# Hybrid decoder layer on one core: the three copies of the sample cache in the queries-and-keys stage wait for later tiles, and a stage's semaphores are cleared behind GpSimd's first work

## The chip, the cores and the metric

The kernel runs on one core of one Trainium2 chip. The metric is the device time of one execution in microseconds (us); lower is better. The times shown are those of three runs of the kernel before; the profile comes from one more execution of it.

## What is computed

One layer of a decoder trunk, in float32, over a prompt of 2048 tokens and a sample of 8 x 4 tokens, of width 1024. What matters here:

```python
h = rms_norm(x, norm1_g) * (1 + sc1) + sh1
z = h @ w_in                                     # q, k, v: 512 columns each; u: 1024
q = rms_norm(q.reshape(B, T, 8, 64), q_norm_g)   # per head
k = rms_norm(k.reshape(B, T, 8, 64), k_norm_g)
o_attn, new_k, new_v = attend(q, k, v)           # three dilated window patterns
...                                              # gated causal convolution of 31 taps on u
x = x + g1 * (concat([o_attn, o_conv]) @ w_o)
x = x + g2 * (square(relu(h2 @ w_ff1)) @ w_ff2)
# sample: the window after appending, an output of the layer
k_all = concatenate([cache_k_l, k], axis=1); new_k_sample = k_all[:, -2048:]
v_all = concatenate([cache_v_l, v], axis=1); new_v_sample = v_all[:, -2048:]
```

The two caches are 8 x 2048 x 512 floats each. All but the first four rows of each sequence go to the output shifted by four rows: 16 copies from DRAM to DRAM, 4088 KB each.

## The kernel before, in words

The program is a row of stages, each a block of its own with one instruction stream per engine: modulation and biases, values and the gated input (VU), queries and keys (QK), prompt attention (PA), sample attention (SA), mixing (MX), feed-forward (FF). A block ends with a barrier over all five engines. GpSimd gathers the other four, releases them, and then clears the semaphores of what has ended (`clear_ended`, L132 to L136: for each range of numbers a drain of GpSimd and a range clear). The other engines don't wait for that.

**Queries and keys** (L1187 to L1460) works tile by tile, 17 tiles: first the 32 sample tokens, then 16 tiles of 128. A float32 product is made of three passes over operands split into a high and a low part.
- TensorE: `products(u)` (L1413 to L1415), 48 matmuls in two halves, each of which adds one to `z_pe`, so that tile u is done at z_pe of 2 (u + 1); behind them `turn_qk(u - 2)` (L1445), 8 transposes of a normed tile into `t_ps`, which wait until ScalarE has taken the turned tile before (`t_done`).
- ScalarE: squares, scaling by head (L1315), then `turned_queries` (L1279) and `turned_keys` (L1291, L1292), which copy turned queries and keys to the buffer `qkT` of two slots. They wait until the store of the tile two before has left its slot (`t_out`).
- VectorE: the norms (L1346 and following), the key gain (L1381), and 9 to 10 us a tile of the prompt's convolution (L307).
- SyncE: for each tile the loads of both parts of h of three tiles on (L1194, 512 KB each), the store of the keys (L1200, 256 KB), the stores of the turned tile (L1214 `qt_d`, L1217 `kt_d`, 192 KB each), and for eight tiles one early load for the next stage (L1238: bias rows, then values of 256 or 1024 KB). It waits in the order in which these stand.
- GpSimd: the sample's convolution, 62 small operations one after the other (L1258 to L1262), then the fourth, fifth and sixth copy of the cache (`copy_cache`, L168 to L174), each behind a wait for `z_pe`. Then it has nothing to do until the stage ends.

**Feed-forward** (L2944 and following) starts with weights and part of h loaded. ScalarE splits off the high part of slot after slot of weights (`high`, L3217) and of h (L3226). GpSimd makes the low parts of the weight slots (`low(s)`, L3159) and of four pieces of h (`h_low(0, 3)`, L3168), VectorE those of four other pieces (L3350) and then the sums for the fast products (L3367 to L3380). TensorE waits for the low part of each slot (`w_lod`) before its matmuls (L3683 to L3685).

Of the kernel before, what the change touches and what calls it, by code (L numbers as in the profile page):

```python
# [94 lines left out]
def build(nc, I, O):  # L95
# [24 lines left out]
    with whole:  # L120
# [11 lines left out]
        def clear_ended():  # L132

            if ended_sems:
                nc.clear_and_free_semaphores(list(ended_sems))
                ended_sems.clear()  # L136
# [31 lines left out]
        def copy_cache(eng, n):  # L168

            b = n // 2  # L170
            for name, out in ((("cache_k", "new_k_sample"), ("cache_v", "new_v_sample"))[n % 2],):
                src = I[name][0, b].rearrange("r h d -> (r h d)")[DS * AW:WINC * AW]
                dst = O[out][0, b].rearrange("r h d -> (r h d)")[0:(WINC - DS) * AW]
                eng.dma_start(dst.rearrange("(a n) -> a n", a=16), src.rearrange("(a n) -> a n", a=16)).then_inc(copied, 16)  # L174
# [62 lines left out]
        with conv:  # L237
# [104 lines left out]
            with ExitStack() as st:  # L342
# [65 lines left out]
                with nc.Block() as block:  # L408
                    @block.gpsimd
                    def _(pool):  # L410
                        pool.memset(ident[:], 0.0).then_inc(id_zero, 1)
                        pool.wait_ge(id_zero, 1)
                        pool.affine_select(out=ident[:], in_=ident[:], compare_op=ALU.not_equal, fill=1.0, base=0,
                                           pattern=[[-1, P]], channel_multiplier=1).then_inc(id_done, 1)
                        pool.wait_ge(tb_done, 3)
                        pool.dma_start(brow_d, biasB[:]).then_inc(tb_out, 16)
                        for g in range(3, NTB):
                            cols = table_cols(g)
                            pool.wait_ge(tb_done, g + 1)
                            pool.dma_start(sbias_d[:, cols], biasS[:, g % 2, 0:cols.stop - cols.start]).then_inc(ps_out[g % 2], 16)  # L420
                        pool.wait_ge(tb_out, 16)
                        pool.wait_ge(ps_out[0], 16 * 2)
                        pool.wait_ge(ps_out[1], 16 * 2)
# [717 lines left out]
            with ExitStack() as st:  # L1141
# [45 lines left out]
                with nc.Block() as block:  # L1187
# [62 lines left out]
                    @block.gpsimd  # L1250
                    def _(pool):
                        step = Chain(pool, tap_d)
                        pool.wait_ge(w_lod, KT)
                        view = lambda t: t[:].rearrange("p c (b t) -> p c b t", t=DS)
                        for j in range(TAPS):
                            w = tapT[:, j * CC:(j + 1) * CC].unsqueeze(2).unsqueeze(3).to_broadcast([P, CC, DB, DS])
                            if j == 0:
                                step(pool.tensor_tensor(view(dwS), gluS[:, :, :, j:j + DS], w, ALU.mult))  # L1258
                                step(pool.tensor_tensor(dwS[:], dwS[:], vecT[:, V_CB:V_CB + CC].unsqueeze(2).to_broadcast([P, CC, NS]), ALU.add))
                            else:  # L1260
                                step(pool.tensor_tensor(view(dwT), gluS[:, :, :, j:j + DS], w, ALU.mult))
                                step(pool.tensor_tensor(dwS[:], dwS[:], dwT[:], ALU.add))  # L1262
                        pool.sem_inc(dw_done, 1)
                        for i in (2, 5, 8):
                            pool.wait_ge(z_pe, 2 * i)
                            copy_cache(pool, 3 + i // 3)

                    @block.scalar
                    def _(act):
# [1402 lines left out]
        with ExitStack() as st:  # L2672
# [147 lines left out]
            def slot_source(eng, s):  # L2820

                b, i = locate(s)
                if b >= BLKS:
                    r = (s - S_OWN) % RAW
                    eng.wait_ge(raw_in[r], 16 * sum(raw_loads(n) for n in range(S_OWN + r, s + 1, RAW)))
                    return flat_glu[:, r * 512:(r + 1) * 512]
                if i < up_slots(b):
                    j, o = divmod(i, PAIR_SLOTS[b])
                    b11, b21, b12, b22 = raw_up(b, j)
                    if is_plain(b):  # L2830
                        raw_ready(eng, b * 4 + j)
                        return (b11, b21, b12, b22)[o]
                    if o in (0, 2, 6):
                        raw_ready(eng, b * 4 + j)
                    else:
                        eng.wait_ge(t_d, 4 * pair_number(b, j) + {4: 1, 3: 2, 1: 3, 5: 4}[o])
                    return (b11, wT[:, 1], b21, wT[:, 2], wT[:, 0], wT[:, 3], b22)[o]
                k = i - up_slots(b)
                U = b * 4 + 2 + k // 4
                raw_ready(eng, U)  # L2840
                return ff_raw[:, U % 2].rearrange("p (f c) -> p f c", f=FB)[:, :, (k % 4) * P:(k % 4 + 1) * P]

            def slot_view(t, s):
                v = t[s % WR]
                b, i = locate(s)
                return v if i < up_slots(b) or b >= BLKS else v.rearrange("p (f c) -> p f c", f=FB)
# [55 lines left out]
            def h_pieces(run, g):  # L2902
                return [(run * HG + g) % 2 * 4 + n for n in range(4)]
# [36 lines left out]

            FIN = {0: 0, 2: 1, 6: 2, 8: 3, 12: 4, 13: 5}

            clear_ended()
            with nc.Block() as block:  # L2944
                @block.sync
                def _(sp):
# [205 lines left out]
                @block.gpsimd  # L3152
                def _(pool):
                    def low(s):
                        if s >= NSLOT:
                            return
                        pool.wait_ge(w_hid, s + 1)
                        src = slot_source(pool, s)
                        pool.tensor_tensor(slot_view(w_lo, s), src, slot_view(w_hi, s).bitcast(F32), ALU.subtract).then_inc(w_lod, 1)  # L3159

                    def h_low(run, g):
                        w = RUNS[run][1]
                        o = {1: 4, 3: 5}[g]
                        for n in range(4):
                            i = h_pieces(run, g)[n]
                            h_ready(pool, run, g, n)
                            pool.wait_ge(ahh_d, 16 * run + 4 * g + n + 1)
                            pool.tensor_tensor(h_lo[o][n][:, 0:w], h_raw[:, i, 0:w], h_hi[o][n][:, 0:w].bitcast(F32), ALU.subtract).then_inc(ahl_p, 1)  # L3168

                    def a_low(e):  # L3170
                        f, tok, w = a_place(e)
                        n = LOW0[e // 8] + e % 8
                        pool.wait_ge(ahi_d, n + 1)
                        pool.wait_ge(sq_d, e + 1)
                        pool.tensor_tensor(a_lo[:, f, tok], z[e % 4][:, 0:w], a_hi[:, f, tok].bitcast(F32), ALU.subtract).then_inc(alo_d, 1)  # L3175

                    def last_low(b):

                        w = RUNS[b // BLKS][1]
                        pool.wait_ge(ahi_d, LOW0[b] + 14)  # L3180
                        pool.tensor_tensor(operand(a_lo, s_lo, "S4", 1, w), seven_source("S4", 1)[:, 0:w],
                                           operand(a_hi, s_hi, "S4", 1, w).bitcast(F32), ALU.subtract).then_inc(alo_d, 1)

                    pool.sem_inc(w_lod, 1)
                    pool.sem_inc(ahl_p, 4)
                    low(1)
                    h_low(0, 3)
                    for s in range(2, WR):
                        low(s)
                    for b in range(NB_ALL):  # L3190
                        run, blk = divmod(b, BLKS)
                        for i in range(up_slots(b)):
                            j, o = divmod(i, PAIR_SLOTS[b])
                            e = 8 * b + 4 * j
                            if is_plain(b):
                                low(SLOT0[b] + i + WR)
                                if o % 2:
                                    a_low(e + o - 1)
                                    a_low(e + o)
                                continue  # L3200
                            low(SLOT0[b] + i + WR)
                        for k in range(DOWN_SLOTS[b]):
                            if blk == BLKS - 1 and run < NR - 1 and k in (1, 3):
                                h_low(run + 1, k)
                            if SEVEN[b] and k == 8:
                                last_low(b)
                            low(SLOT0[b] + up_slots(b) + k + WR)
# [612 lines left out]
```

## Time and profile before

| | |
|---|---|
| median of three runs | 2605.22 us (2602.17 to 2607.79) |
| the profiled execution's own time | 2604.63 us |
| its span in the trace | 2602.8 us |
| TensorE, VectorE, ScalarE, GpSimd busy | 97%, 72%, 49%, 50% of the span |
| mean granted clock of TensorE | 0.985 of full speed |

All times in rows are microseconds from the start of the span. In the profile PE is TensorE (PEld its weight loads), DVE VectorE, ACT ScalarE, POOL GpSimd, SP SyncE; a q behind the name is the engine's instruction queue. The queries-and-keys stage lies at 384 to 610, feed-forward begins at 1237.

### The profile page before, as it was taken

The numbers are of one execution on the slowest core, as the hardware profiler recorded it, in microseconds if no ns is written. First come the engines' busy times: TensorE is split into PE (matmuls) and PEld (weight loads), VectorE is DVE, ScalarE is ACT, GpSimd is POOL, SyncE is SP. The second block draws the span as 40 slices with busy tenths as digits, with TensorE's granted clock in tenths as the row PEclk, the third lists the DMA queues.
The fourth block names the chain that finished last, engine by engine and source line by source line (L and its number), as shares of the span: only waits on it lengthen the run. The fifth ranks groups of instructions, "written<-read, shape, count | busy, mean of one in ns | idle before, by whom it ended". The sixth has DMA issues, their size and how long they took to land. (4 is left out here: it accounts for less than half of the span.)

```text
span 2602.8 us, 46423 instructions
## 1 busy us (share of the span) xinstructions
PE 2515.0 (97%) x16058; PEld 2231.9 (86%) x16058; DVE 1879.3 (72%) x4104; ACT 1281.9 (49%) x3185; POOL 1306.6 (50%) x920
## 2 busy tenths in 40 slices
PE   7999999899999889999899999999999999999998
PEld 4788867687777646887899999999999999999998
DVE  4268898797999647877866666666767786667776
ACT  3443324457888624655434443434555554455553
POOL 0000006006999205664655555556777775677773
PEclk8999999899999999999999999999999999999999
DMA  7866524953445794664456666665555657565443
GB/s 300 289 215 236 205 97 161 302 154 117 136 138 163 271 351 154 190 216 139 150 179 250 235 242 228 211 215 164 183 191 178 193 182 237 167 198 159 144 141 126
DMA packets 362197, 507.84 MB, mean 195 GB/s; under 512 B 29338, under 2 KB 277894, under 8 KB 352102
## 3 DMA queue, kind: packets, MB, share of 16 engines
q1 hardware_dynamic: 340090, 455.45, 53.2%
q0 software_dynamic: 4272, 39.19, 4.3%
q10 hardware_dynamic: 17604, 10.24, 1.3%
q8 instruction: 131, 2.15, 0.3%
q14 instruction: 100, 0.82, 0.1%
HBM read 405.10 MB, written 171.81 MB: 222 GB/s over the span
## 5 line engine op out<-in xcount | busy, mean ns | idle before, releaser
L3159 POOL TENSOR_TENSOR ff_w_lo<-gluT,ff_w_hi 128x512 fp32r<-128x512 f32 x450 | 626.7, 1405 | 319.2 <-ACT ff_w_hi L3217 317.1
L3217 ACT ACTIVATE ff_w_hi<-gluT 128x512 fp32r<-128x512 f32 x450 | 278.7, 626 | 271.6 <-PE ff_u_ps L3685 168.6
L3683 PE MATMUL ff_u_ps<-ff_a_hi,ff_w_hi 128*128 128x352 f32 (+1 forms) x696 | 223.4, 321 | 3.7 <-POOL ff_a_lo L3175 2.5
L3685 PE MATMUL ff_u_ps<-ff_a_hi,ff_w_lo 128*128 128x352 f32 (+1 forms) x696 | 223.0, 320 | 0.0
L3684 PE MATMUL ff_u_ps<-ff_a_lo,ff_w_hi 128*128 128x352 f32 (+1 forms) x696 | 222.5, 320 | 0.0
L1810 ACT ACTIVATE pa_score<-pa_score,pa_stat 128x256 f32<-128x256 f32 (+1 forms) x384 | 172.3, 451 | 30.2 <-DVE pa_stat L1752 27.9
L3683 PE MATMUL ff_u_ps<-ff_h_hi,ff_w_hi 128*128 128x352 f32 (+1 forms) x548 | 176.0, 321 | 1.6 <-DVE ff_u L3567 0.8
L3685 PE MATMUL ff_u_ps<-ff_h_hi,ff_w_lo 128*128 128x352 f32 (+1 forms) x548 | 175.2, 320 | 0.0
L3684 PE MATMUL ff_u_ps<-ff_h_lo,ff_w_hi 128*128 128x352 f32 (+1 forms) x548 | 174.9, 319 | 0.0
L307 DVE SCALAR_TENSOR_TENSOR vu_dwp<-gluT,tapT,vu_dwp 128x512 f32<-128x512 f32 x240 | 161.1, 750 | 0.8 <-DVE rstd L215 0.8
L1025 PE MATMUL vu_z_ps<-vu_w_hi,last_hi 128*128 128x512 f32 (+1 forms) x384 | 152.0, 396 | 0.7 <-DVEq L963 0.7
L1026 PE MATMUL vu_z_ps<-vu_w_lo,last_hi 128*128 128x512 f32 (+1 forms) x384 | 150.3, 392 | 0.0
L1027 PE MATMUL vu_z_ps<-vu_w_hi,last_lo 128*128 128x512 f32 (+1 forms) x384 | 150.0, 391 | 0.0
L3683 PEld LDWEIGHTS ff_u_ps<-ff_a_hi,ff_w_hi 128*128 128x128 f32 x696 | 130.8, 188 | 4.6 <-POOL ff_a_lo L3175 3.0
L3684 PEld LDWEIGHTS ff_u_ps<-ff_a_lo,ff_w_hi 128*128 128x128 f32 x696 | 131.1, 188 | 0.0
L3685 PEld LDWEIGHTS ff_u_ps<-ff_a_hi,ff_w_lo 128*128 128x128 f32 x696 | 130.7, 188 | 0.0
L3159 POOL TENSOR_TENSOR over_acc<-gluT,over_dwq 128x512 fp32r<-128x512 f32 x75 | 104.6, 1395 | 37.1 <-ACT over_dwq L3217 36.4
L3683 PE MATMUL opening_ps<-ff_a_hi,ff_w_hi 128*128 128x352 f32 (+1 forms) x368 | 118.1, 321 | 0.9 <-POOL ff_a_lo L3175 0.9
L3685 PE MATMUL opening_ps<-ff_a_hi,ff_w_lo 128*128 128x352 f32 (+1 forms) x368 | 117.9, 320 | 0.0
L3684 PE MATMUL opening_ps<-ff_a_lo,ff_w_hi 128*128 128x352 f32 (+1 forms) x368 | 117.7, 320 | 0.0
L1650 POOL TENSOR_SCALAR pa_tap_x<-gluT,tapT 128x1024 f32<-128x1024 f32 x40 | 113.9, 2847 | 3.0
L2616 PE MATMUL mx_z_ps<-mx_wo_hi,mx_m_hi 128*128 128x512 f32 (+1 forms) x272 | 110.5, 406 | 0.0
(565 smaller groups left out, 7735.3 us busy)
## 6 DMA issues: line engine op xcount, KB each, us to landing
gluT<-in_w_ff_dram SPq DMA_DIRECT2D x196, 256.0 KB, 3.5
gluT<-in_w_ff_dram SPq DMA_DIRECT2D x64, 512.0 KB, 5.2
gluT<-tu_d SPq DMA_DIRECT2D x112, 256.0 KB, 3.5
gluT<-td_d SPq DMA_DIRECT2D x96, 256.0 KB, 3.2
out_new_k_sample_dram<-in_cache_k_dram SPq DMA_DIRECT2D x40, 511.0 KB, 5.2
out_new_v_sample_dram<-in_cache_v_dram SPq DMA_DIRECT2D x40, 511.0 KB, 5.6
dwq<-in_w_ada_dram SPq DMA_DIRECT2D x32, 512.0 KB, 9.3
gluT<-in_cache_k_dram SPq DMA_DIRECT2D x16, 1024.0 KB, 8.7
```

Source lines behind the costliest of these rows:

```text
L307: return v.scalar_tensor_tensor(out=out, in0=x, scalar=tap(j, c), in1=out, op0=ALU.mult, op1=ALU.add)
L1025: pe.matmul(z, hi, w_hi[:, k, cols], start=k == 0, stop=False)
L1026: pe.matmul(z, hi, w_lo[:, k, cols], start=False, stop=False)
L1027: mm = pe.matmul(z, lo, w_hi[:, k, cols], start=False, stop=k == KT - 1)
L1650: step(pool.tensor_scalar(tap_x[:], gluT[:, c, j + SEQ - LATE:j + SEQ], tap(j, c), None, ALU.mult))
L1810: act.activation(prob[:, u % 4, hh, cols], score[:, u % 4, hh, cols], ACT.Exp, bias=stat[:, p, t, 0, h:h + 1], scale=-1.0, accum_out=stat[ ...
L2616: pe.matmul(z_ps[c][0:n], hi, wo_hi[:, k, cols], start=k == 0, stop=False)
L3159: pool.tensor_tensor(slot_view(w_lo, s), src, slot_view(w_hi, s).bitcast(F32), ALU.subtract).then_inc(w_lod, 1)
L3217: act.activation(slot_view(w_hi, s), src, ACT.Copy).then_inc(w_hid, 1)
L3683: pe.matmul(out, w_hi[s % WR][:, w], hi, start=first, stop=False, skip_group_check=more)
L3684: pe.matmul(out, w_hi[s % WR][:, w], lo, start=False, stop=False, skip_group_check=more)
L3685: return pe.matmul(out, w_lo[s % WR][:, w], hi, start=False, stop=last, skip_group_check=more)
```

## The change

Two edits. In the queries-and-keys stage the waits ahead of the three copies of the cache go from z_pe of 4, 10 and 16 (two, five and eight tiles' products) to 8, 14 and 20 (four, seven and ten tiles'). In feed-forward the clearing of the ended semaphores is no longer emitted ahead of the block but inside GpSimd's stream, behind `low(1)` and `h_low(0, 3)`.

```diff
                         pool.sem_inc(dw_done, 1)
-                        for i in (2, 5, 8):
+                        for n, i in enumerate((4, 7, 10)):
                             pool.wait_ge(z_pe, 2 * i)
-                            copy_cache(pool, 3 + i // 3)
+                            copy_cache(pool, 3 + n)
...
             FIN = {0: 0, 2: 1, 6: 2, 8: 3, 12: 4, 13: 5}
 
-            clear_ended()
             with nc.Block() as block:
...
                     pool.sem_inc(ahl_p, 4)
                     low(1)
                     h_low(0, 3)
+                    clear_ended()
                     for s in range(2, WR):
                         low(s)
```

No engine's instructions change their order in the queries-and-keys stage; only the numbers that the three waits compare with do. This is GpSimd's end of that stage (qk_dwS is the sample's convolution), before and now alike:

```order
L1261 TENSOR_TENSOR qk_dwT<-gluS,tapT 128x128
L1262 TENSOR_TENSOR qk_dwS<-qk_dwS,qk_dwT 128x128
L174 DMA out_new_v_sample_dram<-in_cache_v_dram 64x16352
L174 DMA out_new_k_sample_dram<-in_cache_k_dram 64x16352
L174 DMA out_new_v_sample_dram<-in_cache_v_dram 64x16352
L1187 UNCONDITIONAL_BRANCH
L135 ISA
```

The three copies stand one behind the other, with the stage's end right behind them.

GpSimd at the seam from mixing to feed-forward, of before (ISA at L135 is a range clear, ff_w_lo a weight slot's low part, ff_h_lo a piece of h's):

```order
L2322 DMA x1_d<-mx_x1 32x1024
L2221 UNCONDITIONAL_BRANCH
L135 ISA x2
L3152 UNCONDITIONAL_BRANCH
L3159 TENSOR_TENSOR ff_w_lo1<-gluT,ff_w_hi1 128x512
L3168 TENSOR_TENSOR ff_h_lo<-gluT,ff_h_hi 128x352 x4
L3159 TENSOR_TENSOR ff_w_lo2<-gluT,ff_w_hi2 128x512
L3159 TENSOR_TENSOR ff_w_lo3<-gluT,ff_w_hi3 128x512
```

The same place in the changed program, where the lines of the stage have numbers lower by one up to the new call:

```order
L2322 DMA x1_d<-mx_x1 32x1024
L2221 UNCONDITIONAL_BRANCH
L3151 UNCONDITIONAL_BRANCH
L3158 TENSOR_TENSOR ff_w_lo1<-gluT,ff_w_hi1 128x512
L3167 TENSOR_TENSOR ff_h_lo<-gluT,ff_h_hi 128x352 x4
L135 ISA x2
L3158 TENSOR_TENSOR ff_w_lo2<-gluT,ff_w_hi2 128x512
L3158 TENSOR_TENSOR ff_w_lo3<-gluT,ff_w_hi3 128x512
```

The two clears, each with its drain, moved from ahead of the first weight slot to between the four pieces of h and the second slot; the other engines' streams are as they were.

## Rows read from the trace of the kernel before

**Rows 1.** The page, busy time: engine, us (share), instructions.
```profile
PE 2515.0 (97%) x16058; PEld 2231.9 (86%) x16058; DVE 1879.3 (72%) x4104; ACT 1281.9 (49%) x3185; POOL 1306.6 (50%) x920
```

**Rows 2.** Windows of a tile's length: busy time by engine, granted clock, DMA share, GB/s.
```profile
458.40:470.20 11.80, 10.09 (x45) 8.02 (x43) 11.23 (x22) 0.00 (x0) 0.00 (x0) 1.00 0.91 307
470.20:482.00 11.80, 2.68 (x11) 2.51 (x12) 1.23 (x2) 4.20 (x20) 0.00 (x0) 0.54 1.00 319
...
505.60:517.40 11.80, 11.80 (x58) 9.87 (x57) 10.52 (x20) 4.78 (x20) 0.00 (x0) 1.00 0.86 290
```

**Rows 3.** Timeline of TensorE, L1445: start, us, what, [idle before, releaser].
```profile
456.56 1.03 PE L1445 MATMUL qk_t_ps<-ident,qk_nrm 128*128 128x128 f32 x8
...
479.32 1.94 PE L1445 MATMUL qk_t_ps<-ident,qk_nrm 128*128 128x128 f32 x8 [10.84 <-ACT qk_qkT L1292]
...
493.76 1.03 PE L1445 MATMUL qk_t_ps<-ident,qk_nrm 128*128 128x128 f32 x8
...
505.57 1.03 PE L1445 MATMUL qk_t_ps<-ident,qk_nrm 128*128 128x128 f32 x8
```

**Rows 4.** Timeline of ScalarE, turned queries and keys.
```profile
477.80 0.58 ACT L1279 ACTIVATE qk_qkT<-qk_t_ps,qk_qgain 128x384 f32<-128x384 f32 x1 [19.81 <-DMA kt_d<-qk_qkT]
...
478.68 0.50 ACT L1292 ACTIVATE qk_qkT<-qk_t_ps 128x384 f32<-128x384 f32 x1
...
513.21 0.58 ACT L1279 ACTIVATE qk_qkT<-qk_t_ps,qk_qgain 128x384 f32<-128x384 f32 x1 [6.85 <-DMA kt_d<-qk_qkT]
```

**Rows 5.** Timeline of GpSimd, the three copies as issued.
```profile
446.44 0.56 POOL L174 DMA_DIRECT2D out_new_v_sample_dram<-in_cache_v_dram  x1 [0.63 <-POOL qk_dwS L1262]
447.01 0.50 POOL L174 DMA_DIRECT2D out_new_k_sample_dram<-in_cache_k_dram  x1
494.22 0.50 POOL L174 DMA_DIRECT2D out_new_v_sample_dram<-in_cache_v_dram  x1 [46.71 <-PE qk_z_ps L1415]
```

**Rows 6.** Timeline of SyncE's queue: start, us that the issue took.
```profile
451.08 0.50 SPq L1217 DMA_DIRECT2D kt_d<-qk_qkT  x1
...
457.12 14.62 SPq L1194 DMA_DIRECT2D qk_third_lo<-hs_d  x1
...
476.18 0.63 SPq L1217 DMA_DIRECT2D kt_d<-qk_qkT  x1
```

**Rows 7.** DMA issues near 446.4, 447.0, 476.2, 494.0 and 494.2: size, us to landing.
```profile
out_new_v_sample_dram<-in_cache_v_dram POOLq DMA_DIRECT2D x1, 4088.0 KB, 17.6
...
out_new_k_sample_dram<-in_cache_k_dram POOLq DMA_DIRECT2D x1, 4088.0 KB, 29.4
...
kt_d<-qk_qkT SPq DMA_DIRECT2D x1, 192.0 KB, 7.3
...
last_hi<-hs_d SPq DMA_DIRECT2D x1, 512.0 KB, 3.5
...
out_new_v_sample_dram<-in_cache_v_dram POOLq DMA_DIRECT2D x1, 4088.0 KB, 16.3
```

**Rows 8.** Instructions of L135 from 1236 to 1240: ns min/median/max, first and last start.
```profile
L135 POOLq DRAIN  x2: 71/78/86, 1237.1 to 1237.4; - x2
L135 POOLq EVENT_SEMAPHORE_RANGE_CLEAR  x2: 109/164/218, 1237.2 to 1237.5; - x2
```

**Rows 9.** Timelines of ScalarE, GpSimd, TensorE and VectorE at feed-forward's start.
```profile
1237.32 0.63 ACT L3217 ACTIVATE ff_w_hi<-gluT 128x512 fp32r<-128x512 f32 x1 [5.46 <-PEq L2221]
...
1238.04 1.26 POOL L3159 TENSOR_TENSOR ff_w_lo<-gluT,ff_w_hi 128x512 fp32r<-128x512 f32 x1 [7.56 <-ACT ff_w_hi L3217]
...
1244.29 7.13 POOL L3159 TENSOR_TENSOR ff_w_lo<-gluT,ff_w_hi 128x512 fp32r<-128x512 f32 x5
...
1245.62 0.43 PE L3683 MATMUL ff_u_ps<-over_dwq,ff_w_hi 128*128 128x352 f32 x1 [0.44 <-POOL ff_w_lo L3159]
...
1283.32 0.43 PE L3683 MATMUL ff_u_ps<-ff_a_hi,ff_w_hi 128*128 128x352 f32 x1 [1.27 <-DVE ff_y L3515]
...
1246.31 0.89 DVE L3367 TENSOR_TENSOR ff_e<-gluT 128x352 f32<-128x352 f32 x1 [4.59 <-DMA gluT<-h_d]
```

## Prediction

> **What bounds the kernel now.** I read the page's part on busy time first: TensorE is busy 2515.0 of 2602.8 us [rows 1], so nearly all of what can be won lies in the 88 us in which it stands still or runs slowly, and the question is whether the change touches any of them. The view of waits for the queries-and-keys stage names the line, and the windows of 11.8 us (one tile) show it: from 458.4 TensorE is busy 10.09 of 11.80, from 470.2 only 2.68 at a granted clock of 0.54, where a later tile has 11.80 at 1.00 [rows 2]. The timeline has the cause to the microsecond. TensorE turns a tile's queries and keys (L1445) after each tile of products; undisturbed tiles follow each other in 505.57 - 493.76 = 11.81 us. After 456.56 the next turn was due at 468.4. It began at 479.32, after 10.84 us of idling for ScalarE's L1292, and the one after it at 493.76 [rows 3]. Two tiles took 37.20 us where 23.62 are due: **13.6 us are lost**, 10.9 by standing still and 2.7 because the tile after it began at the lower clock.
>
> ScalarE was not slow: it waited 19.81 us, until 477.80, for a store of turned keys to leave its buffer, and then needed until 479.18 (478.68 + 0.50) [rows 4]. That store was issued at 451.08 and took 26.7 us; SyncE's own queue stood for 14.62 us from 457.12 [rows 6]. What lay ahead of it are two copies of the sample cache, 4088 KB each, issued at 446.44 and 447.01 [rows 5]. They landed 17.6 and 29.4 us later, at 464.0 and 476.4 [rows 7]; the store came free 1.4 us after the second.
>
> Why two at once? The copies stand behind the sample convolution on GpSimd, and that ends only when the first one is issued, at 446.44. By then the waits for z_pe of 4 and 10 (two and five tiles' products; the fifth's ended about 444.8) are long met, so neither holds anything, and only the third copy has a wait of its own, 46.71 us, until 494.22 [rows 5].
>
> **The change, part by part.** *Copies.* The waits become z_pe of 8, 14 and 20, met when the fourth, seventh and tenth tile's products end. In a stage without the loss the products end where the turns begin: 456.56 - 2 x 11.8 = 433.0, 468.4 and 503.8. The first wait is still passed before the convolution ends, so the first copy stays at 446.44. The second moves from 447.01 to 468.4. The third moves by the program's count of tiles two later, from 494.22 to 503.8. Nothing is queued behind them on GpSimd but the end of the stage.
>
> What is left at the first place: one copy. The trace has that case, the third copy: alone, issued at 494.22, it landed after 16.3 us, at 510.5 [rows 5, 7]. ScalarE was then let go at 513.21, after a wait of 6.85 us [rows 4], 19.0 us after the copy's issue, and TensorE lost nothing (11.80 busy of 11.80 from 505.6) [rows 2]. The same 19.0 us after 446.44 give 465.4; ScalarE takes 1.4 us (477.80 to 479.18) and is done at 466.8, 1.6 us ahead of the turn due at 468.4. With the 17.6 us landing in place of 16.3 it is 468.1, just in time. So I take the whole stall as gone: **-13.6**. The second and third copy stand in the same place of a tile as the third does now; by the same 19.0 us ScalarE is free at 487.4 and done at 488.8, against a turn due at 492.0, and for the third at 522.8 and 524.2 against 527.4: **0** each, with 3.2 us to spare. The bounds of this part: 0 gained if the stall merely moves, -13.6 if it goes; a larger gain has no row behind it. The stage's other engines follow TensorE's pace in the undisturbed windows, so I expect the whole of it to reach the end.
>
> *Clearing.* The two drains and two range clears cost 2 x 78 + 2 x 164 ns = 0.48 us, with the gaps between them about 0.6: in front of the block they run from 1237.1 to about 1237.7 [rows 8], while GpSimd has nothing to do: its first work begins at 1238.04, 0.09 us after ScalarE's L3217 ended (1237.32 + 0.63) [rows 9]. So taking them away there gains **0**; the cover is ScalarE's first split. Behind `h_low(0, 3)` they stand ahead of the split of slot 2, at 1244.29, and TensorE does wait for that split: 0.44 us, until 1245.62 [rows 9]. There they cost up to +0.6, since GpSimd runs without a gap up to it. But TensorE stops once more at 1283.32, for 1.27 us, for VectorE, whose chain starts at 1246.31 with a load that was issued ahead of where the clearing now stands [rows 9], so a shift of 0.6 is taken up there. Bounds 0 and +0.6; I take **0**, nearer to the row at 1283.32, and keep +0.6 for the range.
>
> **Sum.** 2604.63 (the profiled execution's own time) - 13.6 + 0 = **2591.0 us**. The median of the three runs shown is 0.6 higher, 2605.22, and they spread over 5.6 us. A difference within 0.2% (5.2 us) can't be told from none.
>
> **A rule weighed.** The store came free only with the copies ahead of it, though it is 192 KB on another queue; a load issued 0.27 us ahead of the third copy landed in 3.5 us [rows 7]. The Trainium skill (DMA: Bandwidth & Descriptors, section Queues, rings and completion order) says that each DMA engine goes round-robin between queues, a packet at a time. By that alone a small store would share the engines and not wait for a copy to end, one copy or two, and pulling the copies apart would change nothing: 2604.6. The trace speaks against it, since the store's release follows the last copy's landing at both places, by 1.4 and 2.7 us.
>
> **Rivals.** *The second copy meets the backlog of the first.* While the copy runs, SyncE is held. Now the following tile's keys are stored at 476.18, 0.2 us before the last copy's landing, and take 7.3 us [rows 6, 7]. With the landing at 462.7 to 464.0 that store goes out at about 462.5 to 463.8 and lands at 469.8 to 471.1, and the second copy is issued at 468.4, in the middle of it. If it is caught it is freed at 487.4, ScalarE is done at 488.8, TensorE's turn due at 480.2 is 8.6 late and the clock costs 2.7: 11.3 of the 13.6 are given back, **2602.3**. For it: the margin is negative. Against it: the load that was issued only 0.27 us ahead of a copy was not caught, and this store is 4.6 us ahead. *Small stalls.* The first copy's margin of 1.6 us is missed, or the 1 MB load of the values takes up the others' 3.2: a stall of 1 to 3 us at one to three places, with slow matmuls after each, **2594 to 2600**. *Nothing changes*, because what a store waits for is SyncE's own backlog (loads of 512 KB and the bias rows), not the number of copies: **2604.6**; against it stands the 26.7 us beside two copies and the shorter wait beside one. *Slower.* The three copies, now spread, each stop TensorE: that takes a store's release more than 22.2 us after the copy's issue at the second and third (19.0 today; the turns are due 23.6 us after it, less ScalarE's 1.4). If each costs what the pair costs now, 3 x 13.6 - 13.6 = +27.2, **2631.8**; with a release a few us over the margin it is some 2610. For it: the values' 1 MB load now runs into the second copy. It needs the landing to be 3 us worse twice, against which stand the 16.3 and 17.6 us of two different places.
>
> **How the numbers follow.** The forecast has 0.74, small stalls 0.08, the caught store 0.07, nothing changes 0.05, slower 0.06. Faster by over 0.2% are the first two: 0.82. Within 0.2%: 0.12. Slower: 0.06. The forecast's own range is 2591.0 with +0.6 for the clearing and about 2.8 us to each side for the spread of runs. Taking in the small stalls gives 2587.5 to 2600.0, which holds 0.82.
>
> **What would show it.** Right: GpSimd's second copy issued near 468.4 and its third near 503.8; L1445 at 456.6, 468.4, 480.2 without an idle row for L1292; granted clock 1.00 from 446.6 on; ScalarE waits of about 7 us for kt_d behind each copy; the stage's last turns and everything behind them 13.6 us earlier; GpSimd's clearing at about 1230.7, with TensorE's wait for slot 2 grown from 0.44 to about 1.0, and its wait for VectorE 38 us later shrunk. Wrong: a wait of TensorE for L1292 at 480.2 (the caught store), or after all three copies.

## The result and the profile after

The changed kernel takes **2587.06 us**, median of five runs (2586.98 to 2593.3), beside 2602.17 for the kernel before in five runs on the same chip (2599.52 to 2607.79). The ratio is 0.9943 [0.9928, 0.9958]. Faster was right, and the forecast of 2591.0 is 3.9 us too high; the measured median lies 0.4 us below the lower end of the range, 2587.5. The profiled execution took 2586.98 us, its span 2585.2.

TensorE's busy time by the page, against [rows 1]:

```profile
PE 2510.4 (97%) x16058; PEld 2229.0 (86%) x16058; DVE 1884.0 (73%) x4104; ACT 1283.0 (50%) x3185; POOL 1302.1 (50%) x920
```

The windows of a tile's length in queries and keys, against [rows 2] (busy us and instructions of PE, PEld, DVE, ACT, POOL, then granted clock, DMA share, GB/s):

```profile
458.40:470.20 11.80, 11.80 (x58) 9.86 (x57) 11.23 (x21) 5.87 (x24) 0.50 (x1) 1.00 1.07 340
470.20:482.00 11.80, 11.80 (x58) 9.86 (x57) 11.23 (x21) 5.75 (x22) 0.00 (x0) 1.00 1.25 435
482.00:493.80 11.80, 11.80 (x58) 9.86 (x57) 11.23 (x21) 4.31 (x20) 0.00 (x0) 1.00 0.82 270
```

The window from 470.2, in which TensorE was busy 2.68 us at a clock of 0.54, now has 11.80 at 1.00. The turns of L1445 on TensorE's timeline, against [rows 3]:

```profile
457.24 1.03 PE L1445 MATMUL qk_t_ps<-ident,qk_nrm 128*128 128x128 f32 x8
...
469.01 1.03 PE L1445 MATMUL qk_t_ps<-ident,qk_nrm 128*128 128x128 f32 x8
...
480.78 1.03 PE L1445 MATMUL qk_t_ps<-ident,qk_nrm 128*128 128x128 f32 x8
...
492.56 1.03 PE L1445 MATMUL qk_t_ps<-ident,qk_nrm 128*128 128x128 f32 x8
```

They follow each other in 11.77 to 11.78 us with no bracket (idle time and what ended it) behind them, so none waited. GpSimd's copies, against [rows 5], and ScalarE's waits for the store of turned keys, against [rows 4]:

```profile
443.38 0.56 POOL L174 DMA_DIRECT2D out_new_v_sample_dram<-in_cache_v_dram  x1 [0.62 <-POOL qk_dwS L1262]
469.48 0.50 POOL L174 DMA_DIRECT2D out_new_k_sample_dram<-in_cache_k_dram  x1 [25.55 <-PE qk_z_ps L1415]
504.79 0.50 POOL L174 DMA_DIRECT2D out_new_v_sample_dram<-in_cache_v_dram  x1 [34.80 <-PE qk_z_ps L1415]
```

```profile
464.46 0.58 ACT L1279 ACTIVATE qk_qkT<-qk_t_ps,qk_qgain 128x384 f32<-128x384 f32 x1 [5.93 <-DMA kt_d<-qk_qkT]
...
489.49 0.58 ACT L1279 ACTIVATE qk_qkT<-qk_t_ps,qk_qgain 128x384 f32<-128x384 f32 x1 [7.91 <-DMA kt_d<-qk_qkT]
```

The second and third copies stand within 1.1 us of 468.4 and 503.8. ScalarE still waits behind them, but its work is done before TensorE needs it.

**Where the time went.** Cut at the barriers between stages (us; Q/K is queries and keys):

```
                        before  before,again  after  after,again
modulation                65.3      63.2       65.1     65.0
values and updates       318.8     316.7      318.8    319.5
Q/K                      225.7     224.7      212.9    212.5
prompt attention         273.0     272.6      272.7    272.7
sample attention          79.8      80.3       78.1     78.4
mixing                   274.5     274.5      271.0    274.6
feed-forward            1365.7    1365.8     1366.6   1366.7
```

The spans differ by 17.6 us, and only 12.8 of these are in the stage where the copies stand; feed-forward gives 0.9 back. Of the rest, 3.5 are mixing's. That isn't the change's: the changed kernel, profiled again, has 274.6 there, and three kernels below that keep the stall (three copies at once, later early loads, copies at the second, sixth and ninth tile) have 270.9 to 271.4. Sample attention's 1.7 isn't either: these three have 78.2 to 78.3, and one kernel with the copies spread has 80.7. Mixing's 3.5 us all lie in its first 38 us. There the kernel before waits for a load of the output weights. TensorE's timeline, kernel before:

```profile
969.02 5.40 PE L2645 MATMUL opening_ps<-gluT 128*128 128x512 f32 x8 [2.12 <-DMA gluT<-in_w_o_dram]
```

The changed kernel waits 0.78 us at this line, for ScalarE. The load is thus part of the difference; the granted clock, 0.68 from 969.0 to 974.4 beside 1.00 in the changed kernel's matching stretch from 952.2, goes with another 1.7. Why the load came late isn't shown.

A pair of profiles thus makes the gain look 5.7 us larger than what the two places of the change give (12.8 - 0.9 = 11.9).

### The profile page after: what moved, and what is told of

The parts are those of the page before. It is cut to its first block and busy times, and to the rows that moved or that the text cites. A ratio compares the mean times of both kernels' runs of the same rounds, so it can differ in the third digit from the quotient of the medians.

```text
span 2585.2 us, 46423 instructions
## 1 busy us (share of the span) xinstructions
PE 2510.4 (97%) x16058; PEld 2229.0 (86%) x16058; DVE 1884.0 (73%) x4104; ACT 1283.0 (50%) x3185; POOL 1302.1 (50%) x920
## 5 line engine op out<-in xcount | busy, mean ns | idle before, releaser
L3683 PE MATMUL ff_u_ps<-ff_a_hi,ff_w_hi 128*128 128x352 f32 (+1 forms) x696 | 223.3, 321 | 3.8 <-POOL ff_a_lo L3174 2.5
L3684 PE MATMUL ff_u_ps<-ff_a_lo,ff_w_hi 128*128 128x352 f32 (+1 forms) x696 | 222.5, 320 | 0.0
L3683 PE MATMUL ff_u_ps<-ff_h_hi,ff_w_hi 128*128 128x352 f32 (+1 forms) x548 | 176.0, 321 | 1.7 <-DVE ff_u L3567 0.8
L3683 PEld LDWEIGHTS ff_u_ps<-ff_a_hi,ff_w_hi 128*128 128x128 f32 x696 | 130.8, 188 | 4.6 <-POOL ff_a_lo L3174 3.1
L3683 PE MATMUL opening_ps<-ff_a_hi,ff_w_hi 128*128 128x352 f32 (+1 forms) x368 | 118.1, 321 | 0.9 <-POOL ff_a_lo L3174 0.9
```

Of the source, the lines that this page charges most:

```text
L3683: pe.matmul(out, w_hi[s % WR][:, w], hi, start=first, stop=False, skip_group_check=more)
L3684: pe.matmul(out, w_hi[s % WR][:, w], lo, start=False, stop=False, skip_group_check=more)
```

## The experiments

Twelve runs: ten kernels, and the two of the comparison once more. Edits are against the kernel before or after, as said. Each ratio is to the kernel before on the same chip.

**One part at a time.** The copies alone (after, with the clearing back in front) and the clearing alone (before, with the clearing moved):

```
 e1: after, with   + clear_ended()          ahead of feed-forward's block
                   -     clear_ended()      behind h_low(0, 3)
 e2: before, with  - clear_ended()          ahead of feed-forward's block
                   +     clear_ended()      behind h_low(0, 3)
```

> The later waits of the three copies alone; the clearing stays ahead of feed-forward. Theory (the whole gain is the copies'; the clearing costs a little): 13 to 15 us less than before, ratio 0.9942 to 0.9950; the queries-and-keys stage about 212.9 us from barrier to barrier as in the changed kernel, feed-forward 1365.7 as in the kernel before, so 0.9 us faster there than the changed kernel. Rival (the clearing brings part of the 15.1): only some 10 to 12 us less, and mixing back at 274.5 us.

> The moved clearing alone; the copies wait as before. Theory: the 13.6 us stall is there (10.8 us idle before the turn at 479), feed-forward 0 to 1 us longer, time 0 to 1 us over before, ratio 1.000 to 1.0004. Rival (the clearing brings part of the gain): 2 to 5 us less than before.

Measured: copies alone 2589.57 us (six runs, 2584.62 to 2593.79), ratio 0.9955 [0.9943, 0.9967]; its Q/K stage takes 212.9, feed-forward 1365.8. Clearing alone 2602.44, ratio 1.0005 [0.9996, 1.0014]; Q/K 225.4, feed-forward 1368.1. The copies' gain is 12.1 us by these medians, a little less than I expected, and in the stage's length it is the changed kernel's. With the clearing alone TensorE's stall was 9.90 us, and feed-forward grew by 2.4 us where I had expected 0 to 1. The gain is the copies', all of it as far as whole runs can tell; what the clearing does is under that, and is read from the traces further down.

**Both kernels again**, unchanged, for the spread of stages (the table above):

> The kernel before, once more, for the length of each stage. Theory (the 1.7 us in sample attention and 3.5 us in mixing by which the changed kernel's profile is shorter are differences between executions): sample attention or mixing comes out 1 to 4 us away from the 79.8 and 274.5 of the first profile; queries and keys again 225.7 within 1, with the stall. Rival (they belong to the change): 79.8 and 274.5 within 0.5.

> The changed kernel, once more. Theory: queries and keys again 212.9 within 1 and no idle row for L1292 behind the copies; sample attention and mixing spread over 77 to 80 and 270 to 275. Rival: 78.1 and 271.0 within 0.5, apart from the kernel before.

Measured: before 2599.56, after 2591.15. Before's stall of TensorE was 10.3 us instead of 10.8, and two tiles took 36.0 us instead of 37.2. The loss at this place is thus 12.4 to 13.6 us, not one number. My expectation for the other stages was missed by the kernel before: its sample attention and mixing came out within 0.5 us of the first profile. That they belong to no part of the change is shown by the other profile, and by all fourteen together, in which mixing lies between 270.4 and 274.6 and sample attention between 78.1 and 82.3.

**Three copies at once** (before, with the third copy's wait put at five tiles too):

```
-                        for i in (2, 5, 8):
+                        for n, i in enumerate((2, 5, 5)):
...
-                            copy_cache(pool, 3 + i // 3)
+                            copy_cache(pool, 3 + n)
```

> Waits of 2, 5 and 5 tiles: all three copies issued one behind the other at about 446.4 to 447.6. Theory (the store of turned keys comes free about 2 us after the last copy issued ahead of it lands, and TensorE stands until then): the third lands some 12 us after the second, near 489, TensorE idles about 23 us before the turn due at 468.4 instead of 10.8, the queries-and-keys stage is 237 to 239 us, the time 11 to 13 us over before, ratio about 1.005. Rival (TensorE's stall comes from SyncE's own backlog of loads): the stall stays at 10.8, the time as before.

Measured: 2613.96, ratio 1.0048 [1.0031, 1.0064], Q/K 235.8. TensorE's timeline:

```profile
487.23 1.94 PE L1445 MATMUL qk_t_ps<-ident,qk_nrm 128*128 128x128 f32 x8 [21.71 <-ACT qk_qkT L1292]
```

One more copy, 10.9 us more of idling: the stall goes with the number of copies that stand together. Two cost 10.8, three 21.7, and one nothing, because one fits into ScalarE's slack.

**Without SyncE's own early loads** (before, with the loads of bias rows and values begun at tile 6 instead of 3):

```
-                            if 3 <= u < 3 + len(first_loads):
-                                dst, src = first_loads[u - 3]
+                            if 6 <= u < 6 + len(first_loads):
+                                dst, src = first_loads[u - 6]
```

> Kernel before with SyncE's early loads for the next stage (L1238) begun three tiles later, so that neither the bias rows nor the values' 1 MB load stand in SyncE's queue beside the pair of copies. Theory: the idle before the turn at 479 stays within 2 us of 10.8, the stage at 224 to 226. Rival (SyncE's own backlog holds the store): it shrinks to below 5 us.

Measured: 2596.58 in one run, TensorE idle 8.34 us before the turn, Q/K 223.3: just outside my expectation, and far from the rival's. So these early loads hold about 2 us of the stall. The run leaves the loads of h where they are; that SyncE's loads as a whole are not the cause is shown by the kernels with spread copies, which have them all and no stall.

**No copies worth the name** (after, with each of the three cut to 512 of its 65,408 elements per row, 32 KB; the rest of the sample's values of sequence 1, and of keys and values of sequence 2, is not written):

```
+                eng.dma_start(dst[:, 0:512], src[:, 0:512]).then_inc(copied, 16)
...
-                            copy_cache(pool, 3 + n)
+                            copy_little(pool, 3 + n)
```

> The changed kernel with only 32 KB of each of the stage's three copies left (rows of new_k_sample and new_v_sample for sequences 1 and 2 are not written). Theory (spread copies cost TensorE nothing): queries and keys 212.8 us within 0.5, as with the copies, ScalarE's three waits of about 7 us for kt_d gone; the time within 1 to 2 us of the changed kernel's. Rival (spread copies still cost): the stage, or sample attention behind it, is shorter by over 1 us.

Measured: 2588.68, ratio 0.9957 [0.9943, 0.9971], Q/K 212.5, where the kernels with spread copies have 212.5 to 212.9. Spread, the copies cost nothing, and nothing more is to be had here.

**How near is too near?** (before, with the copies at the second, sixth and ninth tile)

```
-                        for i in (2, 5, 8):
+                        for n, i in enumerate((2, 6, 9)):
...
-                            copy_cache(pool, 3 + i // 3)
+                            copy_cache(pool, 3 + n)
```

> Waits of 2, 6 and 9 tiles: the second copy is issued at 456.6, 10 us behind the first and 12 before where the change puts it. Theory (only what is issued behind a copy waits for it): the store issued at 451 comes free near 466, the turn due at 468.4 is on time; the next tile's store, issued near 462, is held to the second copy's landing near 476 to 478, so that the turn due at 480.2 is 0 to 2 us late; the stage 213 to 216 us, the time 10 to 13 us under before. Rival (what counts is the copies' bytes in flight, whenever issued): a stall of 8 to 11 us as in the kernel before, stage 223 to 226.

Measured: 2598.75, ratio 0.9997 [0.9987, 1.0006]: nothing gained. This is the first clear miss of the series. The copies stood 10.7 us apart and the stall was whole. Timelines of GpSimd, ScalarE and TensorE in that kernel:

```profile
444.94 0.56 POOL L174 DMA_DIRECT2D out_new_v_sample_dram<-in_cache_v_dram  x1 [0.62 <-POOL qk_dwS L1262]
455.62 0.50 POOL L174 DMA_DIRECT2D out_new_k_sample_dram<-in_cache_k_dram  x1 [10.12 <-PE qk_z_ps L1415]
...
475.82 0.58 ACT L1279 ACTIVATE qk_qkT<-qk_t_ps,qk_qgain 128x384 f32<-128x384 f32 x1 [19.33 <-DMA kt_d<-qk_qkT]
...
477.35 1.94 PE L1445 MATMUL qk_t_ps<-ident,qk_nrm 128*128 128x128 f32 x8 [10.27 <-ACT qk_qkT L1292]
```

and the DMA issues between 448 and 456.5, size and us to landing:

```profile
kt_d<-qk_qkT SPq DMA_DIRECT2D x1, 192.0 KB, 26.3
...
out_new_k_sample_dram<-in_cache_k_dram POOLq DMA_DIRECT2D x1, 4088.0 KB, 18.8
```

The store was issued at 449.48, the second copy 6.1 us *later*, at 455.62, and still the store landed at 475.8, 1.4 us after that copy (455.62 + 18.8 = 474.4). A copy therefore holds a store that is already on its way. "Ahead of it" in my working was wrong; what counts is whether the store is through when the second copy starts to move.

**Why a 192 KB store waits for 8 MB.** The counts of packets give it. DMA queues in the stretch 454.5 to 471.5: packets, MB, share of 16 engines, in the kernel before (q0 carries the copies, q1 the loads and stores of SyncE):

```profile
q0 software_dynamic: 107, 5.95, 103.8%
q1 hardware_dynamic: 107, 0.22, 3.6%
```

One against one: 107 packets of the copies, by the records 91 of 65,408 bytes and, where the first copy ends, 16 of 4 bytes, and 107 packets of the rest, 2048 bytes each, worth 0.22 MB. From 460 to 465, first the kernel before, beside its copies, then the changed one, whose first copy has landed (443.4 + 15.6 = 459.0) and whose second hasn't begun:

```profile
q0 software_dynamic: 43, 1.77, 104.0%
q1 hardware_dynamic: 44, 0.09, 5.2%
```

```profile
q1 hardware_dynamic: 1389, 1.90, 104.2%
```

44 packets against 1389 in the same time. The single records show an engine taking 2.4 to 4.0 us for one packet of a copy, 3.0 at the median. A store of 512-byte pieces has 24 packets per engine, so beside a copy its queue gets one through in about 3 us, and in effect the store waits until the copies have no packets left. The records show it: not one 512-byte packet begins before 473.6, and the copies' last long packet began at 472.7; until then their queue was passing the 2048-byte packets of the key store ahead of them. This is what the Trainium skill states (DMA: Bandwidth & Descriptors, Queues, rings and completion order): an engine goes round-robin between queues, a packet at a time. The counts agree with it, 107 to 107. In the prediction I drew from this rule that a small store would not have to wait; that was the wrong conclusion from a right rule, since turns are equal in packets, and by the counts 27 times unequal in bytes (5.95 MB against 0.22).

If so, shorter packets must change the stall. Two kernels cut the copies' rows (before, the pair left at one place):

```
+            cut, by = ("(a n) -> a n", dict(a=16)) if n < 3 else ("(b a n) -> a b n", dict(a=16, b=146))
...
-                eng.dma_start(dst.rearrange("(a n) -> a n", a=16), src.rearrange("(a n) -> a n", a=16)).then_inc(copied, 16)
+                eng.dma_start(dst.rearrange(cut, **by), src.rearrange(cut, **by)).then_inc(copied, 16)
```

and the same with b=32.

> The kernel before, its pair of copies at the third tile kept, but each of the three copies in queries and keys cut into rows of 1792 bytes (146 on each of 16 DMA engines) instead of 65408 bytes (4 on each). Theory, packet turns: in the trace of before, of the stretch 454.5 to 471.5, the copies' queue and the queue of loads and stores each moved 107 packets, one of 65408 bytes against one of mostly 2048, so a store waits one copy packet of about 3.1 us for each packet of its own. Behind the first copy's start some 56 packets an engine stand up to the end of kt_d's store (8 of 2048 bytes of new_k_prompt, 24 and 24 of 512 bytes of qt_d and kt_d). With turns of 1792 bytes, estimated at 0.2 to 0.25 us for a pair of packets, they are through after 11 to 14 us, so the store issued at about 451 lands by 465, TensorE doesn't wait before the turn after the fourth tile (in before it did for 10.8 us), the stage of queries and keys takes 213 to 217 us, and the ratio to before is 0.995 to 0.997. Rival, bytes: stores wait until the copies' 8.4 MB are through, however these are cut: the wait of 10.8 us stays, the stage takes 225 us, ratio 1.000. Third: the short rows make the copies slower and the loads behind them too, and the stage is longer than 226 us.

> As the one with rows of 1792 bytes, but rows of 8176 bytes, 32 on each engine and copy, 64 for the pair. Theory, packet turns: some 56 packets of stores stand against 64 turns of the copies, so nearly the whole pair still goes ahead of kt_d's last packet: the store lands 1 to 4 us earlier than in before (473 to 477), TensorE still waits 6 to 10 us, the stage takes 221 to 225 us. If turns are given by bytes and not by packets, the wait is that of before, 10 to 11 us, and is the same in the kernel with 1792 bytes. If long packets as such are the trouble, it is gone here as well.

Measured, rows of 1792 bytes: 2596.59, ratio 0.9986 [0.9974, 0.9998], Q/K 222.5. DMA queues from 454.5 to 471.5, and TensorE's turn:

```profile
q0 software_dynamic: 969, 5.09, 82.6%
q1 hardware_dynamic: 967, 1.16, 19.7%
```

```profile
478.56 1.94 PE L1445 MATMUL qk_t_ps<-ident,qk_nrm 128*128 128x128 f32 x8 [7.31 <-ACT qk_qkT L1292]
```

Rows of 8176 bytes: 2610.04 in one run, Q/K 230.9, the same views:

```profile
q0 software_dynamic: 514, 4.07, 75.5%
q1 hardware_dynamic: 509, 1.08, 27.0%
```

```profile
484.12 1.94 PE L1445 MATMUL qk_t_ps<-ident,qk_nrm 128*128 128x128 f32 x8 [14.46 <-ACT qk_qkT L1292]
```

Equal turns hold in all three, at packets nine and five times as many: 107 to 107, 969 to 967, 514 to 509. Both sizes of my expectations were missed. With short rows the relief is 3.5 us and not 10.8, since three rows of 1792 bytes go as one packet: the records have 5376 bytes. A turn took 17 x 16 / 969 = 0.28 us, near the estimate, but at 5376 bytes the pair still has some 100 turns per engine in place of 292, and the queue ahead of the store had loads in it that I hadn't counted: 256 packets of 4096 bytes, two loads of h, went between 450 and 459, where the kernel before had them through by 449.4. That makes 72 packets per engine up to the store's end and not 56. The store landed at 477.0, 4.8 us *before* the second copy (448.02 + 33.8 = 481.8): with more turns than packets ahead of it, a store does pass a copy. With 8176 bytes the stall grew by 3.6 us instead of shrinking. The pair has 64 turns there, fewer than the 72 packets (the same 256 of 4096 bytes stood ahead, from 451 to 462), each 17 x 16 / 514 = 0.53 us and shared with a packet of SyncE's, and its second copy lands after 35.9 us instead of 29.4 [rows 7], with the store still behind it: it was issued at 451.82 and landed at 482.5, 30.7 us. The rival "bytes" falls with the first (a stall that changes with the cut), my amounts with both; equal turns are shown by the counts.

**Just behind the store** (after, second copy at half of the seventh tile, by 13 halves instead of 14):

```
-                        for n, i in enumerate((4, 7, 10)):
-                            pool.wait_ge(z_pe, 2 * i)
+                        for n, i in enumerate((8, 13, 20)):
+                            pool.wait_ge(z_pe, i)
```

> The changed kernel, but the second copy waits for the first half of the seventh tile's products (about 463.3) and not for the whole of it (469.5); the first copy's landing is at about 459 to 461 then, and kt_d's store lands at 464.5 where nothing comes between. The second copy's first packets come 2 us behind its issue, as the records of before and after have it, so at about 465. Theory, packet turns: what decides is whether the store is through when these packets start; it is, by half a us to a us, and the stage takes 213 us, with no wait of TensorE over 1 us before the turns. If what held the store in the kernel with the copies at the second, sixth and ninth tile was merely that the second copy was issued while it was pending, this one is caught too: the store lands at 476 to 480, ScalarE waits over 18 us, and the stage takes 224 us.

Measured: 2597.11 in one run, Q/K 216.7. ScalarE's waits for the store:

```profile
465.52 0.58 ACT L1279 ACTIVATE qk_qkT<-qk_t_ps,qk_qgain 128x384 f32<-128x384 f32 x1 [6.56 <-DMA kt_d<-qk_qkT]
482.21 0.58 ACT L1279 ACTIVATE qk_qkT<-qk_t_ps,qk_qgain 128x384 f32<-128x384 f32 x1 [11.04 <-DMA kt_d<-qk_qkT]
```

The second copy went out at 464.65. The first store landed at 465.5, and was not held, as expected. The *next* one was: issued at 464.34, it landed only at 482.2, TensorE stood still for 2.19 us before its turn, and the stage was 3.8 us longer than with the whole tile. I had looked at one store and not at the one that follows it. In the changed kernel that store, issued at 463.71, takes 5.6 us and is through at 469.3; the copy goes out at 469.48, and its first packets begin at 471.9. In its second profile the store landed at 470.3, 0.6 us behind the copy's issue at 469.71, and wasn't held either: what it must beat is the copy's first packets, which here came 3.4 us behind the issue (468.1) and still met the store.

**The clearing, moved on** (after, with the clearing behind GpSimd's first round of low halves):

```
-                    clear_ended()
                     for s in range(2, WR):
                         low(s)
+                    clear_ended()
```

> The changed kernel, but GpSimd's clearing of semaphores in feed-forward is moved on behind the first round of six low halves instead of behind its first work. Theory: in the changed kernel the clearing's some 0.5 us of drain and clear delay the low halves that TensorE's second products wait for, so feed-forward takes 1366.6 to 1368.1 us instead of 1365.6 to 1366.0; here GpSimd has these ready before it clears and is idle for 1.6 us afterwards, so feed-forward takes 1365.5 to 1366.0 and the whole 0.9 to 2 us less than the changed kernel, 2585 to 2588, ratio to before 0.994 to 0.995. Rival: the longer feed-forward is the spread of its barrier and not GpSimd's, and stays at 1366.6 or more.

Measured: 2587.24, ratio 0.9943 [0.9928, 0.9957], the same as the changed kernel's; feed-forward 1365.8. First GpSimd and TensorE in the changed kernel, then GpSimd in this one:

```profile
1226.55 7.11 POOL L3158 TENSOR_TENSOR ff_w_lo<-gluT,ff_w_hi 128x512 fp32r<-128x512 f32 x5 [0.76 <-issue]
...
1227.88 0.43 PE L3683 MATMUL ff_u_ps<-over_dwq,ff_w_hi 128*128 128x352 f32 x1 [0.79 <-POOL ff_w_lo L3158]
...
1265.62 0.43 PE L3683 MATMUL ff_u_ps<-ff_a_hi,ff_w_hi 128*128 128x352 f32 x1 [1.27 <-DVE ff_y L3515]
```

```profile
1237.67 1.40 POOL L3158 TENSOR_TENSOR over_acc<-gluT,over_dwq 128x512 fp32r<-128x512 f32 x1 [0.77 <-issue]
1239.69 1.60 POOL L3158 TENSOR_TENSOR ff_w_lo<-gluT,ff_w_hi 128x512 fp32r<-128x512 f32 x1 [0.62 <-ACT ff_w_hi L3217]
```

Behind the first work the clearing opens a gap of 0.76 us ahead of the split of slot 2, and TensorE's products of L3683 start 0.8 us later, counted from the stage's first split, than in the copies-only kernel: at the 20th of them, and still at the 1500th. All five kernels profiled with the clearing at that place have 0.8 at the 20th and 0.7 to 1.0 at the 1500th, and of the nine others none has more than 0.4 at the 20th; the wait for VectorE is 1.27 us as before and took nothing up. Two of the five (clearing alone, and the second copy at half a tile) got a further 1.5 us behind the 1500th product, which the other three did not; where from stays open. One kernel with the clearing in front, the one with rows of 8176 bytes, lags as well, by 0.3 at the 20th product and 0.8 from the 150th on: a lag of this size can have another source. Moved behind the round, the same 0.77 eats into ScalarE's slack, whose wait falls from 1.63 us (kernel before, at 1254.58) to 0.62; the lag is 0.3 us at the 20th product and under 0.1 from the 150th on, and the kernel before, profiled again, has 0.4 and none with its clearing in front. So 0.8 us are won, by this one trace; whole runs don't resolve it, and this version beats the kernel before as the changed one does, not the changed one.

## Why the prediction was right, and where it failed

- **The stall and its cause held.** Two copies at once, a store of turned keys behind them, ScalarE, TensorE: taken apart by the copies alone (0.9955), three at once (1.0048) and none (0.9957). What TensorE still waits in the changed stage, 4.7 us at its first products and 4.2 at its last turn, it waits in the kernel before too.
- **Its size was a little high.** -13.6 was one profile's. Executions of the pair lost 12.4 to 13.6 us at this place, and the stage went from 225.7, 224.7 and 225.4 to 212.5 to 212.9: about **-12.6**.
- **The clearing was mis-sized.** I took 0, with +0.6 as a bound; by the traces it is **+0.8**. The step that failed here is that "a shift of 0.6 is taken up" at TensorE's wait for VectorE at 1283.32 [rows 9]. That chain's input was issued early, but its end moved along with the rest. The 0 in front of the block was right: feed-forward is not shorter for it.
- **The sum's level and the width of the range failed, and this is what put the measured time outside the range.** Mechanism and direction were right; the failed step is the level of the sum, its first term and the nothing for the stages outside the change. The sum took one execution's 2604.63 as the level, and put all that happens outside the two places of the change at nothing. Between the two profiled executions the other stages differ by 5.7 us (mixing 3.5, sample attention 1.7, the rest 0.5), and with that term the sum closes: 2604.63 - 12.8 + 0.9 - 5.7 = 2587.0, measured 2586.98. For the medians, terms as measured give 2604.63 - 12.6 + 0.8 = 2592.8, further off than the forecast, whose two misses in the terms (1.0 and 0.8 us, both towards too fast) hid part of the level's. Of the 5.7 us between 2592.8 and 2587.06 the base makes 2.5: 2604.63 belongs to one execution, while the five runs beside the changed kernel have a median of 2602.17, and later groups of 14 to 17 runs of the same kernel 2599.64 to 2601.69. Against 2602.17 the same terms give 2590.4. The other 3.3 us lie within the changed kernel's own scatter, and what made them up is open, as only one of its five runs has a profile; that one, 0.1 us from the median, has mixing's short form. The changed kernel's runs span 2586.98 to 2593.3, the copies-only kernel's 2584.62 to 2593.79.
- **The width.** "About 2.8 us to each side for the spread of runs" allowed for the scatter of one side only; the three runs shown already had 5.6 between them, and the base's error comes on top. The terms named don't give the lower end either: 2591.0 - 2.8 is 2588.2, and not 2587.5. The ratio's interval, times 2602.17, is -18.7 to -10.9 us, and holds both -13.6 and -11.8.
- **Rivals.** The caught store is a real mechanism: the kernel with copies at the second, sixth and ninth tile shows it in full, and the half-tile kernel in part. My argument against it, that the load issued 0.27 us ahead of a copy was not caught, proved little: that load landed at 497.45, and by the records the copy's first packet began at 496.57, 2.35 us behind its issue. What saved the changed kernel is that kt_d's store of the next tile was through 2.6 us before the copy's first packets, and 2.7 in its second profile. No row of the prediction had that margin, so the conclusion was right on a weak reason, and partly by luck. "Nothing changes" rested on SyncE's backlog, of which the early loads hold 2 of the 13 us; with the copies spread or cut away and every load in place the stall is gone. "Slower" needed releases over 22.2 us after a copy's issue at the second and third; they came at 489.49 - 469.48 = 20.0 and, by ScalarE's wait that ends at 524.97, at 20.2, against the 19.0 that I had. With ScalarE's 1.4 us TensorE's turns at 492.56 and 527.88 had 1.7 and 1.5 us to spare, and not 3.2.

## What to carry to other kernels

- A large DRAM-to-DRAM copy in long packets gave the other queue one packet per turn here, and small stores on the path then waited for its end, even if they were issued first. Start such a copy right after the stores that matter have landed, not merely at a distance from the other copies, and look at the next tile's stores too.
- When a wait is meant to space work out, look in the trace whether it is ever waited on: here two of three had been met long before GpSimd came to them.
- Forecast the difference place by place from one profile, but take the level, and its width, from all runs of the kernel before, and leave room for stages that the change doesn't touch.

## What the hardware showed that I had not expected

- Cutting the copies into rows of 8176 bytes made the stage 5.2 us *longer* than with 65,408 (230.9 against 225.7), as the second copy needs 35.9 us in place of 29.4: 3.6 us more at the stall, and a second stop of 1.3 us before the turn at 522.94, behind the third copy alone. At 5376 bytes per packet (rows of 1792) it needs 33.8, and the stall shrinks to 7.3 us. In these two kernels the store passed the copies where its queue had fewer packets left than they had turns (72 against some 100), and not where it had more (72 against 64).
- The drain and clear of semaphores, 0.48 us by their own durations [rows 8], cost GpSimd 0.76 to 0.77 us of its time at either place, and TensorE 0.8 at the 20th product where nothing covered them.
- Mixing takes 271.0 and 274.6 us in two profiles of the same kernel, and between 270.4 and 274.6 in all fourteen. A late load of the output weights is part of it, and not all: the shortest, 270.4, waited 1.34 us for it.
